# A chunked linear recurrence on one core: inverse by two products a level instead of three, without crossed products

## The reference

```python
def wkv7_scan(r, w, k, v, a, b, reverse):
    ...
    def step(S, inp):
        r_t, w_t, k_t, v_t, a_t, b_t = inp
        sa = jnp.einsum('bhij,bhj->bhi', S, a_t)
        S = S * w_t[:, :, None, :] + sa[..., None] * b_t[:, :, None, :] + v_t[..., None] * k_t[:, :, None, :]
        return S, jnp.einsum('bhij,bhj->bhi', S, r_t)
...
    for d, reverse in enumerate((False, True)):
        ...
        wkv = wkv + wkv7_scan(rh, heads(decay), kd, vh, -kk, kk * ah, reverse)
```

## Time and profile before

| | us |
|---|---|
| median of 3 runs | 2392.42 |
| lowest, highest | 2386.65, 2393.29 |
| the profiled execution's own time | 2391.54 |
| its span, first to last instruction | 2389.7 |
| PE, DVE, ACT busy in the span | 2180.5, 671.2, 319.5 |
| granted PE clock, mean | 0.955 |

### The profile page before, as it was taken

One profiled execution on the slowest core, in us unless ns is written; L12 is line 12 of the kernel. 1 busy time (PEld: TensorE's weight loads), 2 busy tenths in 40 slices (PEclk: granted clock), 3 DMA queues, 4 the chain that ended last, 5 costly groups with the idle time before them and its releaser, 6 DMA issues. The chain is left out here.

```text
span 2389.7 us, 47609 instructions
## 1 busy us (share of the span) xinstructions
PE 2180.5 (91%) x22006; PEld 1318.7 (55%) x22006; DVE 671.2 (28%) x1247; ACT 319.5 (13%) x717; POOL 23.3 (1%) x21
## 2 busy tenths in 40 slices
PE   6999999999999999999999999899976998777676
PEld 5778888887634444353534344678766862222121
DVE  6863222345401101101101102455454432111110
ACT  2431000144100000000000000333132110000000
POOL 1000000000000000000000000000000000000000
PEclk9999999999999999999999999999999998777877
DMA  9668554802599999999999999433300579999998
GB/s 400 246 255 343 212 211 202 336 2 103 241 402 400 419 405 419 402 420 401 420 392 419 398 419 418 176 124 138 132 3 5 235 310 421 422 421 422 421 421 361
DMA packets 111471, 734.64 MB, mean 307 GB/s; under 512 B 12768, under 2 KB 16128, under 8 KB 36640
## 3 DMA queue, kind: packets, MB, share of 16 engines
q1 hardware_dynamic: 109328, 724.55, 74.9%
q0 software_dynamic: 1152, 4.19, 0.4%
q10 hardware_dynamic: 784, 2.75, 0.3%
HBM read 721.33 MB, written 10.09 MB: 306 GB/s over the span
## 5 line engine op out<-in xcount | busy, mean ns | idle before, releaser
L1550 PE MATMUL bank<-ring,moe_xg 128*32 128x512 f32 (+1 forms) x6144 | 581.8, 541 | 0.7 <-DVE moe_xg L1706 0.7
L1550 PEld LDWEIGHTS bank<-ring,moe_xg 128*32 128x32 f32 x6144 | 199.2, 110 | 378.0 <-issue 375.9
L1561 PE MATMUL bank<-ring,moe_turned 128*32 128x256 f32 x5376 | 291.5, 379 | 0.0
L1561 PEld LDWEIGHTS bank<-ring,moe_turned 128*32 128x32 f32 x5376 | 174.7, 110 | 117.1 <-issue 3.1
L1104 PE MATMUL bank<-h_chan,ring 128*128 128x256 f32 x896 | 195.6, 379 | 1.4 <-ACT h_chan L505 1.4
L1104 PEld LDWEIGHTS bank<-h_chan,ring 128*128 128x128 f32 x896 | 170.2, 190 | 24.6 <-issue 1.6
L2055 PE MATMUL bank<-ring,late 128*32 128x512 f32 x696 | 120.5, 792 | 52.3 <-DMA ring<-stream 52.3
L1745 DVE TENSOR_TENSOR moe_hidden<-moe_silu,bank 128x512 f32<-128x512 f32 (+1 forms) x48 | 26.9, 617 | 482.8 <-PE bank L1550 482.8
L2502 PE MATMUL bank<-h_chan,ring 128*128 128x256 f32 x672 | 148.0, 380 | 1.9 <-DVE h_chan L2607 1.9
L2502 PEld LDWEIGHTS bank<-h_chan,ring 128*128 128x128 f32 x672 | 127.1, 190 | 23.0 <-issue 6.3
L2055 PEld LDWEIGHTS bank<-ring,late 128*32 128x32 f32 x696 | 17.7, 122 | 150.2 <-DMA ring<-stream 129.3
(11 more groups left out here) (463 smaller groups left out, 2043.2 us busy)
## 6 DMA issues: line engine op xcount, KB each, us to landing
ring<-stream SPq DMA_DIRECT2D x257, 1024.0 KB, 22.8
ring<-wide SPq DMA_DIRECT2D x240, 1024.0 KB, 15.6
ring<-wide SPq DMA_DIRECT2D x128, 768.0 KB, 15.6
late<-stream SPq DMA_DIRECT2D x47, 1024.0 KB, 27.0
ada_slots<-stream SPq DMA_DIRECT2D x28, 1024.0 KB, 7.2
h_chan<-stream SPq DMA_DIRECT2D x9, 1024.0 KB, 26.7
rows<-zeros SPq DMA_DIRECT2D x8, 512.0 KB
moe_x_rows<-rows SPq DMA_DIRECT2D x28, 96.0 KB, 8.2
```

What stands on the lines that cost most here:

```text
L1550: mm = self.k.nc.tensor.matmul(banks[r][i * TILE:(i + 1) * TILE, 0:width], self.m.xg[:, r, t * TILE:(t + 1) * TILE], w[:, i, :], start=(t ...
L1561: mm = self.k.nc.tensor.matmul(self.sum_bank[r][q * TILE:(q + 1) * TILE, :], self.m.turned[:, r, n * TILE:(n + 1) * TILE], w[:, f2, q * T: ...
```

## The change

The inverse is found from a *step* and a *front* for each chunk, a matrix and its transpose in nature: `step` is what is to be multiplied next, (I+N) times the inverse so far, masked to the blocks of the next level (the identity is in the mask), and `front` carries its transpose, unmasked. A level is two products for a chunk: one into `front_bank` (step and front) (not at the last level), copied by ACT, and front x step into `full_bank`, masked by DVE (L3287 in the changed file). After level 5 the mask is half of the strict upper triangle plus the identity, and what DVE writes then is the inverse itself. The mask table shrinks from 1216 to 960 columns.

All products are now kept products. `both`, `turn` and the transposed inverse are gone. The transposes and masked products are the same 24, 4 more masked products start the inversions of chunks 2 and 3, and each kind alternates between two banks. There are 106 products: 8 for starting the four inversions, 44 in their levels, 24 transposes and masked products, and 30 in the tail. The second pair's levels are placed between the tail's products of chunks 0 to 2. The loads before the stage, the merge and everything after are as they were.

The diff, cut to its core:

```diff
-        LEAD, EXTRA_FILL = (1, 0), (3, 2)
-        FILLS = ((0, 2, 4, 5), (1, 3, 4, 5))
+        ROWS = (("v", 0), ("v", 1), ("k", 0), ("k", 1), ("b", 0), ("b", 1), ("v", 2), ("v", 3), ("k", 2), ("k", 3),
+                ("b", 2), ("b", 3))
+        MASKS = (("ak", 0), ("rk", 0), ("ak", 1), ("rk", 1), ("rb", 0), ("rb", 1), ("front", 2), ("step", 2), ("ak", 2),
+                 ("rk", 2), ("front", 3), ("step", 3), ("ak", 3), ("rk", 3), ("rb", 2), ("rb", 3))
+        ROWS_AT, MASKS_AT = (4, 6, 8, 10, 12, 12), (2, 4, 8, 12, 14, 16)
...
-                inversion(0)
-                inversion(1)
...
+                for c in range(2):
+                    for kind, bank in (("front", front_bank[c]), ("step", full_bank[c])):
+                        product(bank, *lead_parts(kind, c)).then_inc(*lead_done.up())
+                for j in range(4):
+                    row(j)
+                for level in range(LEVELS):
                     for s in range(2):
...
+                        level_step(0, level, s)
+                    for j in range(ROWS_AT[level - 1] if level else 4, ROWS_AT[level]):
+                        row(j)
+                    for j in range(MASKS_AT[level - 1] if level else 0, MASKS_AT[level]):
+                        mask(j)
+
+                x_own(0)
+                for s in range(2):
+                    level_step(1, 0, s)
+                solve(0)
+                s_own(0)
+                for s in range(2):
+                    level_step(1, 1, s)
+                s_solved(0)
+                y_own(0)
+                y_solved(0)
+                x_own(1)
...
+                for s in range(2):
+                    level_step(1, 5, s)
+                x_state(2)
+                s_own(2)
+                s_state(2)
+                solve(2)
+                y_own(2)
+                y_state(2)
+                s_solved(2)
+                y_solved(2)
+                x_own(3)
+                x_state(3)
+                y_own(3)
+                solve(3)
+                y_state(3)
+                y_solved(3)
...
+                def lead(kind, c, bank, signal):
+                    dst, part = (front[c], masked(6)) if kind == "front" else (step[c], masked(0))
+                    link(v.tensor_tensor(dst, bank, part, ALU.mult))
+                    v.tensor_tensor(dst, dst, unit, ALU.add).then_inc(*signal.up())
...
+                def steps(p, level):
+                    for s in range(2):
+                        dve.wait_ge(*level_done.at(level_at(p, level, s)))
+                        v.tensor_tensor(step[2 * p + s], full_bank[s], masked(level + 1 if level < LEVELS - 1 else 7),
+                                        ALU.mult).then_inc(*step_out.up())
```

More of the change, by code:

```diff
@@ L3063, in values, with product @@
             return pick
[L3065 to L3071, removed]
+        def product(bank, a, b, first=True, last=True):
             for n in range(8):
                 for half in range(2):
-                    mm = matmul(bank, a, b, n, half, turn, first, last)
+                    rows = head_slice(half)
+                    mm = nc.tensor.matmul(bank[rows, n, :], a(rows, n), b(rows, n), start=first and n == 0,
+                                          stop=last, skip_group_check=True)
@@ L3076, in product, with turned @@
             return mm
-        def both(kept, turned, kept_last=True):
+        def turned(bank, a):
             for n in range(8):
                 for half in range(2):
[L3082 to L3103, removed]
+                    rows = head_slice(half)
@@ new lines, in turned, with level_at, front_at, lead_parts @@
+                    mm = nc.tensor.matmul(bank[rows, n, :], a(rows, n), ident[rows, rows], start=n == 0, stop=True, skip_group_check=True)
+            return mm
+        def level_at(p, level, s):
+            return 12 * p + 2 * level + s + 1
+        def front_at(p, level, s):
+            return 10 * p + 2 * (level - 1) + s + 1
+        def lead_parts(kind, c):
+            A, B, R, K = (of(cut(t, c)) for t in (at, bt, rt, kt))
+            return {"front": (A, B), "step": (B, A), "ak": (K, A), "rk": (K, R), "rb": (B, R)}[kind]
@@ L3230, in _ @@
-                one, _ = both((*solve(1), True, True), (*y_own(2), True, False))
-                one.then_inc(*z_done.up())
-                product(*y_state(1), first=False, last=False)
-                pe.wait_ge(*z_out.at(2))
-                product(*s_solved(1), first=False).then_inc(*state_done.up())
-                product(*y_solved(1), first=False).then_inc(*y_done.up())
-                pe.wait_ge(*state_out.at(2))
-                product(*x_state(2), first=False).then_inc(*x_done.up())
@@ new lines, in _ @@
+                y_own(1)
+                y_state(1)
+                for s in range(2):
+                    level_step(1, 4, s)
+                s_solved(1)
+                y_solved(1)
+                x_own(2)
+                for s in range(2):
+                    level_step(1, 5, s)
[7 more added lines that the diff above has]
+                y_solved(2)
@@ L3311, in outputs @@
                 def outputs(c):
-                    bank = y_bank[c % 2]
                     dve.wait_ge(*y_done.at(c + 1))
@@ L3348, in _ @@
[L3348 to L3354 removed]
+                for c in range(2):
+                    for i, (kind, bank) in enumerate((("front", front_bank[c]), ("step", full_bank[c]))):
+                        dve.wait_ge(*lead_done.at(2 * c + i + 1))
+                        lead(kind, c, bank, lead_out)
@@ new lines, in _ @@
+                for level in range(LEVELS):
+                    steps(0, level)
+                    for j in range(MASKS_AT[level - 1] if level else 0, MASKS_AT[level]):
+                        mask(j)
+                steps(1, 0)
+                gains(0)
+                gains(1)
+                steps(1, 1)
+                new_state(0)
+                outputs(0)
+                steps(1, 2)
+                gains(2)
+                gains(3)
+                steps(1, 3)
+                steps(1, 4)
```

319 lines of the change are left out of this document (122 added, 197 removed).

## The result

The changed kernel takes 2374.7 us, the median of 4 runs (2373.22 to 2376.19), against 2391.56 for the kernel before (4 runs). The ratio is 0.9933 with a 95% interval of 0.9916 to 0.995, that is 12 to 20 us less. A later set on one chip gave 0.9926 (0.9913 to 0.9938) for the same file. The profiled execution took 2373.22 us.

A forecast was written before the change was run, and what follows sets the result against it. The prediction took a chain of engine handovers to bound the recurrence, and the weight stream behind it the end. 99.6 us of products plus 1.1 of waits against 115.6 saves 14.9, so 2391.54 becomes 2377 us, range 2371 to 2385.

The forecast's parts named there:

- The stage's sum: Recurrence of the changed kernel: 99.6 us of products plus 1.1 us of open handovers, 100.7 us against 115.6.
- What bounds the end: End of kernel: streaming the last mixture's weights, which starts after the recurrence, so the recurrence's 14.9 us gain reaches the end.
- The price of a single product: PE in the recurrence: 0.94 us for each product issued alone, 106 products making 99.6 us.
- the one wait: PE ahead of `x_own(0)`, after the last masked product: nothing stands between, so 1.0 us idle.
- No engine fills it, so it is bound by a chain: Recurrence before: PE busy 80.7 of 115.8 us, handovers between engines set its time, 44.2 us of it waiting.
- The turned product was free: Paired products before: a kept and a turned product together take 0.95 us, as long as one alone.
- the covers: New order in the recurrence: other products between producer and consumer hide handovers of 0.90 us (ACT) or 1.0 us (DVE).
- S: Theory formed after the result, not forecast: PE's instruction supply, 14.4 ns each, bounds the stage before, 8064 instructions in 115.8 us.
- Part of the waits stays: First rival, chance 0.11: DVE between two chains holds steps back, 5 to 9 us return, time 2382 to 2386.
- PE's work grows and the waits stay: Rival, chance 0.04: 24 level steps leave PE idle 1.5 us each, stage 135.6 us, kernel 2411.6 us.
- Turns at the bank: Rival, chance 0.01: by the skill's Gotcha 1, row halves take turns at a PSUM bank; product 1.88 us, kernel 2476.
- The gain hidden: Rival, chance 0.03: what paces the end already flows beside the recurrence, so the end stays at 2391.5 us.

The follow-up runs named there:

- Experiment 4: Kernel before, DVE doing each of the 20 masks of W V twice: stage 116.2 us. Likewise kernel after, 24 step masks twice: stage 101.35 us.
- experiment 1: Kernel before with the 16 transposes and masked products beside W V at levels 2 to 5 left out: stage 103.9 us, whole 2376.62 us.
- experiment 2: Kernel after with 22 more products, each crossed with one of chunk 0's or 2's level products: stage 121.0 us.

## Why the prediction was right, and where it was not

**The time.** 2377 forecast, 2374.7 measured, in the range of 2371 to 2385. The stage's sum was 100.7 us and it takes 101.0; the gain was to be 14.9 and is 14.8 in the stage. The medians lie 16.9 apart; what is beyond the stage's 14.8 comes from stretches where the code is the same, and the runs of one kernel scatter by more than that (2386.65 to 2393.29 before).

**What bounds the end** held. The stream starts behind the stage, nothing flows beside it, and 14.8 us came through. The other runs agree: the whole moved with the stage, to within some 5 us in single runs, where executions of the kernel before scatter from 2387.65 to 2397.23 (the run with 32 columns can't be used for it).

**The price of a single product**, 0.94 us, held: 54 products in 50.8 us. So did the place and size of the one wait (1.0 said, 0.88 found). The two small waits between masks (0.1 us together) did not show. DVE's 43 us held (42.99), and its order held nothing back. That the handovers of the new order are covered held even with 0.7 us added to each.

**"No engine fills it, so it is bound by a chain" failed.** That is the step from the earlier trace rows. At three of its six instructions in the earlier trace rows DVE did wait some 2 us for PE (at the others 0.2 us or not at all, where the prediction's first rival says "nearly every instruction"), but PE was not waiting for DVE. Of PE's 35 idle us, 33.4 had no releaser, and by the experiments PE stood without instructions in them. DVE's idle time shows that DVE is not the bound; what PE waited for stood in PE's own waits, which weren't read. Experiment 4 on the kernel before shows it most directly: longer handovers moved the stage by 0.4 us, where this step asks for 7 to 14.

**"The turned product was free" failed.** Rows 6 and 7 show that a pair takes no more *time in the array* than a single product, and that is true within a burst. Over a stretch longer than a burst, a product costs 64 instructions at 14.4 ns, 0.92 us, crossed or not. Measured, a crossed product cost 0.74 us (experiment 1) and 0.91 us (20.0 / 22, experiment 2).

**Why the number came out nevertheless.** The sum for the kernel after needed only the price of a single product and the covers. The price in the array, 0.935 us, and the price in the supply, 0.90 to 0.92 us, lie close together here, so it didn't matter which of them binds. That is luck. The kernel before entered with its measured time, so that a wrong reason for its waits couldn't harm the sum. Read by S, the change is 1280 instructions fewer, 18.4 us at 14.4 ns, of which the array's own pace and the 0.88 us wait take back 3.6. The prediction would have gone wrong for a variant with paired products: it would have called 22 crossed products free, where they cost 20 us.

**Readings that were off, with nothing resting on them.** On the page, PE's low slices are the 30th and 31st, and DMA is at 0 in the same two, not in 31 and 32. The 9.3 us between PE's busy 80.7 and the 71.4 of issuing are put down to ends of 0.2 us at each wait; with the 25 gaps that the trace has, that makes 5 us. So the 44 us of waiting are 35 us of idle time and 9 us in which PE is busy by the profile.

**The rivals.** Part of the waits stays: no. PE's work grows and the waits stay: no. Turns at the bank: no, 0.94 us a product throughout. Whether two row tiles may write the same partitions of a bank at one time, which the rule named there may mean, no run here shows. The gain hidden: no. None of the rivals named what the kernel before had, an engine that waits for its own instructions.

## What to carry to other kernels

Before calling a stage bound by a chain, read the waits of the engine that the chain is said to hold, and not only those of its partners: idle time with no releaser, in bursts of equal count, points to the instruction stream. In small-matmul code, count instructions beside array time; in this kernel, packing two products into idle quadrants asked for 128 instructions in the 0.94 us in which some 64 came in, and it bought next to nothing. Dropping instructions did pay; merging them paid 40% of what was expected. An order that is written by hand to cover handovers is worth testing against the plain one, which here was only 0.5 us slower.

## What the runs showed of the hardware

In the recurrence PE's instructions arrived as packets of 16 KB, 31 in 115.8 us before and 26 in 101.0 us after. Where PE ran out of them, there was one per burst of 127 or 128 matmuls with their weight loads, and the bursts shown are 3.3 to 4.1 us apart. Within a burst PE ran two products crossed in 0.94 us, 7.3 ns an instruction, twice the mean. In the kernel before, where one burst follows another, a packet began 1.0 to 1.5 us after the burst had begun (at 1767.54 for the one from 1766.10), took 1.15 us in the mean of the 31, and the next burst began 1.3 to 1.5 us after the packet's end. These parts add up to the distance of the bursts. Whether it is the time of one fetch with only one under way, or something behind it, no run separates. Every execution on record has a span and a clock from the profiler; whether the supply is the same without it, no run shows either.

It was also not expected that the supply would be a little faster where PE's work was small: 14.0 ns in the run with 32 columns against 14.4 in the kernel before. (The forms with all products alone, 14.7 to 15.0 ns, stand at the array's price and don't bear on it.)
